# A table of expert gates in another memory layout: long runs where it is read, 256-byte pieces where it is written

## The reference, cut to what matters

```
s1, i1 = top_k(s[:, :, 0], 16);  s2, i2 = top_k(s[:, :, 1], 16)   # two keys of 128 each
sc, ic = top_k(s1[..., :, None] + s2[..., None, :], 16)
idx  = e1 * 128 + e2                                   # expert number
gate = softmax(sc)
act  = gelu(einsum('td,thkd->thk', xb, u[idx]))
out  = einsum('thk,thkd->td', gate * act, v[idx])
```

## Time and profile before

| | us |
|---|---|
| median of 3 runs (lowest, highest) | 4213.85 (4208.09, 4213.94) |
| the profiled execution, its own time | 4209.01 |
| its span, first to last instruction | 4207.4 |
| PE busy (share of the span) | 4016.6 (95%) |
| DVE busy | 3169.2 (75%) |
| ACT busy | 1439.4 (34%) |
| POOL busy | 1307.2 (31%) |

### The profile page before, as it was taken

How to read it: one execution, slowest core, us unless ns; L and a number is a source line. 1 busy time by engine, 2 the same in 40 slices (tenths; PEclk the granted TensorE clock), 3 DMA queues, 4 the chain that set the end, 5 groups by cost and what they waited for, 6 DMA issues and landing times.

```text
span 4207.4 us, 82817 instructions
## 1 busy us (share of the span) xinstructions
PE 4016.6 (95%) x30898; PEld 3663.9 (87%) x30898; DVE 3169.2 (75%) x6289; ACT 1439.4 (34%) x2563; POOL 1307.2 (31%) x1014
## 2 busy tenths in 40 slices
PE   8999999997689999999999998999999999999998
PEld 5998887786559979888888878999999999999997
DVE  5721424555762378887889888999999999999998
ACT  4212222223552132333378872222222222222223
POOL 5333331000121100344433324434434334444341
PEclk9999999999889999999999999999999999999999
DMA  6765675574833311344446669999999999999995
GB/s 223 228 200 192 204 241 191 227 264 127 231 115 96 125 54 39 103 143 144 142 153 206 222 222 337 298 301 300 302 302 301 300 299 300 300 300 301 303 300 191
DMA packets 532581, 928.46 MB, mean 221 GB/s; under 512 B 286849, under 2 KB 355201, under 8 KB 524817
## 3 DMA queue, kind: packets, MB, share of 16 engines
q1 hardware_dynamic: 396512, 549.91, 40.7%
q0 software_dynamic: 81056, 346.96, 24.6%
q10 hardware_dynamic: 54816, 28.85, 2.4%
HBM read 786.05 MB, written 206.30 MB: 236 GB/s over the span
## 4 chain that ended last, share of the span: by engine, by line
PE 42%; DMA 3%; DVE 2%; ACT 2%; SPq 1%; issue 0%; DVEq 0%; ACTq 0%
PE ex_pso L3728 19%; PE ex_psa L2951 19%; PE wte_psa L2951 3%; DMA eg_u<-in_u 2%; PE wt_ps L3468 1%; DVE wt_one L3417 1%; DVE wt_stage L3429 0%; ACT eg_u_high L3044 0%; DMA weights<-wt_stage 0%; ACT wt_one L3496 0%; ACT wt_stage L3503 0%; DVE wt_one L3421 0%; ACT eg_act L3071 0%; SPq L3378 0%; ACT wt_one L3495 0%
## 5 line engine op out<-in xcount | busy, mean ns | idle before, releaser
L3696 POOL DMA_INDIRECT ex_rows<-expert_rows,ex_here x512 | 588.4, 1149 | 953.5 <-DVE acc_tok L3936 864.0
L3936 DVE SCALAR_TENSOR_TENSOR acc_tok<-ex_rows,ex_wsp,acc_tok 128x1024 f32<-128x1024 f32 x512 | 635.1, 1283 | 0.0
L2951 PE MATMUL ex_psa<-x_dense_high,eg_u_high 128*128 128x288 f32 x2048 | 604.4, 295 | 7.1 <-DVEq L4050 6.3
L2951 PE MATMUL ex_psa<-x_dense_low,eg_u_high 128*128 128x288 f32 x2048 | 604.5, 295 | 0.0
L2951 PE MATMUL ex_psa<-x_dense_high,eg_u_low 128*128 128x288 f32 x2048 | 604.2, 295 | 0.0
L3050 POOL TENSOR_TENSOR eg_u_low<-eg_u,eg_u_high 128x1024 fp32r<-128x1024 f32 x130 | 314.2, 2417 | 742.1 <-ACT eg_u_high L3044 742.1
L3815 ACT ACTIVATE ex_w<-ex_psa 128x288 f32<-128x288 f32 x256 | 105.2, 411 | 1057.3 <-PE ex_psa L2951 1057.3
L3728 PE MATMUL ex_pso<-ex_w_high,ex_v_high 128*128 128x288 f32 x2048 | 442.4, 298 | 18.2 <-DVE acc L3918 16.6
L3728 PE MATMUL ex_pso<-ex_w_high,ex_v_low 128*128 128x288 f32 x2048 | 440.5, 297 | 0.0
L3728 PE MATMUL ex_pso<-ex_w_low,ex_v_high 128*128 128x288 f32 x2048 | 439.1, 296 | 0.0
L3918 DVE TENSOR_TENSOR acc<-ex_pso,acc 128x576 f32<-128x576 f32 x512 | 375.4, 754 | 44.8 <-PE ex_pso L3728 44.8
(11 more groups left out here) (577 smaller groups left out, 8799.2 us busy)
## 6 DMA issues: line engine op xcount, KB each, us to landing
eg_u<-in_u SPq DMA_DIRECT2D x256, 512.0 KB, 5.6
expert_rows<-in_v SPq DMA_DIRECT2D x128, 512.0 KB, 7.0
ex_v<-in_v SPq DMA_DIRECT2D x128, 512.0 KB, 6.4
weights<-wt_stage SPq DMA_DIRECT2D x36, 1024.0 KB, 4.9
ex_g<-weights SPq DMA_DIRECT2D x128, 288.0 KB, 6.7
expert_rows<-eg_act SPq DMA_DIRECT2D x256, 128.0 KB, 1.7
proj<-in_out POOLq DMA_DIRECT2D x50, 548.5 KB, 6.4
in_w<-in_w_in SPq DMA_DIRECT2D x50, 512.0 KB, 5.1
```

The costliest lines, as they stand in the source:

```text
L2951: yield nc.tensor.matmul(out[:, 0:b - a], w[:, kc, :], half[:, kc, a:b], start=n == 0, stop=n == len(passes) - 1)
L3696: pool.indirect_dma_start(rows[i][:, :], None, table, index(here[par][:, t, j:j + 1]), element_offset=ROW_RUNS[t][0]).then_inc(s_row[i], 16)
L3936: v.scalar_tensor_tensor(out=acc_tok[:, t, :], in0=rows[i][:, at:at + D], scalar=wsp[:, i:i + 1], in1=acc_tok[:, t, :], op0=ALU.mult, op1= ...
```

## The change

The table `weights` in memory was (token block, e2, e1, token) and becomes (e2, e1, token block, token). A load of one group's gates for one partition was 9 runs of 256 bytes, and is one run of 2304 bytes. A stored piece for one partition was one run of 8192 bytes, and is 32 runs of 256 bytes that lie 2304 bytes apart. The bytes moved and the number of DMA instructions are the same, and on every engine the instructions keep their places: 36 stores and 128 loads change their shape.

```
@@ store_piece
-                    sp.dma_start(io["weights"][b][:, f, :].rearrange("e f t -> e (f t)"),
-                                 stage[slot][:, f, :].rearrange("p f t -> p (f t)")).then_inc(s_st[slot], 16)
+                    sp.dma_start(io["weights"][:, f, b, :], stage[slot][:, f, :]).then_inc(s_st[slot], 16)
@@ load_gates
-                        sp.dma_start(g[s][:, :, :], io["weights"][:, :, sl, :].rearrange("b p e t -> p b (e t)")).then_inc(s_g[s], 16)
+                        sp.dma_start(g[s][:, :, :].rearrange("p b t -> p (b t)"), io["weights"][:, sl, :, :].rearrange("p e b t -> p (e b t)")).then_inc(s_g[s], 16)
@@ program
-                            ("weights", (NTB, NK, NK, TB)), ("expert_rows", (NK, NK, ROW))):
+                            ("weights", (NK, NK, NTB, TB)), ("expert_rows", (NK, NK, ROW))):
```

## The result

| | before | after |
|---|---|---|
| median, us | 4213.9 | 4256.38 |
| lowest to highest, us (4 runs each) | 4208.09 to 4219.23 | 4249.62 to 4258.13 |
| ratio, 95% interval | | 1.0098, 1.0082 to 1.0114 |
| profiled execution's span, us | 4207.4 | 4256.0 |

The change makes the kernel 42.5 us slower where 27 were forecast. The time lies in the stated range. The two spans differ by 48.6 us, and ACT's gelus divide them. The one ahead of the first stored block comes 3.6 us later after (2175.34 and 2178.98); 3.0 of these are there already at 2036 us, where the change has no part. From it to the last gelu of gate building it is 333.4 us before and 375.1 after, 41.7 more. From there to where PE runs without a break (2573.20 and 2621.77) it is 64.5 and 67.7, 3.2 more. Behind that nothing differs.

The account below looks back on a forecast made before the run. PE was taken to bound the loop and gate building. A loss of 24 us in gate building plus 2.7 in the transition, on the median 4213.9, gave 4241 us, range 4213 to 4268.

Parts of the forecast that it names:

- The steady loop: The loop after the transition: PE waits for nothing in 25.5 us a pair of groups, so shorter loads give nothing.
- A piece takes 2.3 us more: Stores in gate building and transition: 1.05 MB in 256-byte runs takes 4.8 us instead of 2.5.
- The DMA share: In gate building, the DMA share was to rise from 0.65 to about 0.85.
- ACT's waits: In gate building, ACT's wait for `eg_u` was to grow from 20.2 to about 55 us.
- PE's loss: In gate building, PE loses 3.7 us a block, 3.0 more than before; 24 us over eight blocks.
- the lead of 1.9: In gate building, DVE runs 1.9 us ahead of PE, which is taken off the delay that reaches PE.
- The transition: From gate building to the loop: it ends 2.7 us later, bounds 0 to 9.2.
- two terms of 9.2 and 6.5: In the transition, the four last pieces take 9.2 us more; DVE's idle of 6.52 us goes.
- The range: Whole kernel 4213 to 4268 us; the forecast's own range 4224 to 4268 allowed stage 10 to 45, transition 0 to 9.
- The rule on packets of queues taking turns: In the transition, loads' small packets alternate with gathered packets, so `eg_u` lands after 31.84 us; under 10 after the change.
- The estimate of 3.4 us for a piece: By the skill's descriptor cycles, a stored piece takes 0.9 us more and the kernel's sum is near no change.

Follow-up runs that it names:

- the runs with one late turn: Kernel before with only piece 0, or only piece 3, of each block stored twice in long runs: 4213.44 us and 4224.76 us.
- double_fourth: Kernel before with only piece 3 of each block stored twice in long runs: 4224.76 us, ratio 1.0045.
- double_store: Kernel before with each of the 32 pieces of gate building stored twice in long runs: 4255.01 us, ratio 1.0107.
- loads_alone: Kernel before with only the loads changed to one 2304-byte run per partition, stores still 8192-byte runs: 4203.24 us, ratio 0.9983.

## Why the prediction was right, and where its sizes were off

- **The steady loop: nothing.** Right: 3013 matmuls in 400 us before and after, at a DMA share of 0.88.
- **A piece takes 2.3 us more, and `eg_u` is there 9.6 us after the gelu.** Right: the two loads of the rows above are there 9.5 us (2337.10) and 10.2 us (2345.01) after the end of the gelu ahead of their issue (2327.60 and 2334.79), and the landing of `eg_u` has its median at 7.9 us (5.6 before), the forecast's number. The median of a piece is 6.6 us (4.8 before, 6.8 forecast). The DMA share did not follow: 0.85 was forecast and it is 0.69 in the block shown.
- **ACT's waits.** Forecast 2.4, 2.5, 0 and 1.9 us in turns 1 to 4; measured 2.7, 2.8, 0.5 and 1.7; in all 61.3 us (about 55 forecast).
- **PE's loss: the mis-sized term.** "Less the lead of 1.9" made it 0.8, 2.2 and 0.7 us in turns 1, 2 and 4; it was 1.8, 2.6 and 1.1, and 0.3 in turn 3. For the stage 24 us were forecast and 41.7 came. The lead had been read as DVE's wait less PE's, 2.51 - 0.59. The 0.59 counts from the end of the matmul record before, and these records run 0.39 us though one starts every 0.23. The weight load of the same matmul had waited longer:

```profile
2324.86 0.39 PE L2951 MATMUL wte_psa<-x_gathered_low,eg_u_high 128*128 128x512 f32 x1
2325.09 0.39 PE L2951 MATMUL wte_psa<-x_gathered_high,eg_u_low 128*128 128x512 f32 x1
2326.07 0.53 PEld L3468 LDWEIGHTS wt_ps<-wt_one 128*128 128x128 f32 x4 [1.02 <-DVE wt_one L3417]
```

That gives 1.5, and the means of all blocks before give 2.4 - 1.2 = 1.2 us; the runs with one late turn have 1.4 and 1.0. With 1.2 in the forecast's own sum, turn 1 would have lost 1.5, turn 2 2.2 and turn 4 1.1, less the 1.3 lost before (not 0.7): 3.5 a block, 28 us. So the lead is a small part of the miss. DVE's waits, up to 0.4 us longer in turns 1 and 2 than forecast, and turn 3, which lost 0.3, bring the weight loads' waits to what the table has: 4.6 us a block more than before, 36.7 in the stage.
- **The clock: a term that the sum did not have.** The gelus drift by 5.2 us a block, 0.6 more than those waits. Windows of the stage before, the stage after, and a stretch of it, with the matmuls there:

```profile
2175.34:2508.70 333.36, 327.13 (x1656) 274.54 (x1655) 298.44 (x634) 289.38 (x729) 112.98 (x47) 1.00 0.63 212
2178.98:2554.07 375.09, 338.70 (x1656) 278.96 (x1655) 298.67 (x634) 289.06 (x728) 112.36 (x47) 0.98 0.67 188
2247.50:2251.00 3.50, 3.50 (x11) 2.76 (x11) 2.85 (x7) 1.89 (x6) 0.06 (x1) 0.51 0.80 252
```

```profile
2246.98 0.78 PE L3467 MATMUL wt_ps<-wt_one 128*128 128x256 f32 x4 [2.38 <-DVE wt_one L3416]
2247.56 0.62 PE L2951 MATMUL wte_psa<-x_gathered_high,eg_u_high 128*128 128x512 f32 x1
2247.98 0.63 PE L2951 MATMUL wte_psa<-x_gathered_low,eg_u_high 128*128 128x512 f32 x1
```

Before, the granted clock was 1.00 all through the stage. After, it stood at 0.5 (1.2 GHz) in five stretches, each beside a wait of PE of 2.4 to 3.1 us; the longest such wait before was 1.4. In these stretches 29 matmuls of the early groups start 0.43 us apart instead of 0.23: 5.7 us, 0.7 a block, about what was left over. The same sum nearly closes the other runs: weight loads' waits and slow matmuls give 16.7 + 2.1 for 19.0 us in double_fourth and 35.9 + 8.0 for 45.7 in double_store. That PE's waits bring the clock down is read from rows that lie together; other waits of over 2 us had no such stretch beside them, and no run varied the clock alone.
- **The transition: 2.7 us, by two terms of 9.2 and 6.5.** The sum was 3.2, and the terms were others. DVE's first row slot came 13.0 us later, not 9.2, since SP's held issue kept every engine back, which the forecast did not have: SP had issued the last piece 17.75 us after the last gelu (5.16 before), 12.6 later. The pieces themselves landed 7.1 us later (2578.79 less 2554.07, the issue of the gates' load less the last gelu, against 17.6). DVE's own stretch gave back 9.8 us, not 6.5: the prediction called it free of other gaps, and it had five waits for gathered rows, 2.7 us in all, which went too. With them PE's waits for DVE's adds fell from 16.6 to 6.7 us, where the prediction had them stay. The two errors nearly cancel. That is luck, and the right sum proves neither term.
- **The range.** The time lies in it, but with the stage at 41.7 us of the 45 that it allowed; its centre was too low.
- **The rule on packets of queues taking turns.** In loads_alone the `eg_u` of the earlier trace rows is used 9.1 us after its issue (2537.68 to 2546.78) instead of landing after 31.84, DVE's idle of 6.52 us is gone, and the transition is 3.5 us shorter. The trace agrees with the Trainium skill (DMA: Bandwidth & Descriptors, "Queues, rings and completion order"), by which an engine takes turns between the queues packet by packet; the turns themselves are not seen in a row.
- **The estimate of 3.4 us for a piece**, worked out from the same page's cycles per descriptor ("Why small descriptors are slow"), is 308 GB/s, near the stretch at 290 and far from the one at 218. The kernel did not come out near no change, as the sum by that page had it.

## What to carry to other kernels

A transfer's price is not only its own time: look at what is queued behind it, and at who waits for that. Here four pieces a block, for which nobody waits, made the loads behind them land 2.3 us later; that cost 5.2 us a block, and moving one line of the issue order gave it all back and more. Before making a load in a PE-bound loop cheaper, ask which wait ends last there; before making a store dearer, measure the slack of the chain behind it, and read it from the weight load's wait, not from the matmul's. When the engine that sets the pace begins to wait, look at its granted clock too: here 5.7 of 41.7 us went there.

## What the runs showed of the hardware that was not expected

- Stores in 256-byte runs ran at two steady rates in one stretch, 290 and then 218 GB/s (14.1 and 18.8 ns a packet and engine), both with packets under 512 bytes of one queue alone. The times of the packets add up to 127.5% of the engines' span in 2561 to 2565 us and to 85.6% in 2567 to 2571. 512-byte runs had 347 GB/s. What switches between the rates was not tried.
- SP is through with a DMA of 4096 runs after 0.38 us, but is then held 3.9 us at the next DMA, and 15.3 us over four in a row; with 128 runs each it was 2.7 us. What holds it no row names. At the end of a part of the program this holds the other engines too: ACT starts 0.90 us after SP's last issue, before and after.
- TensorE's granted clock was at 0.5 in five stretches of the changed kernel's stage, each beside a wait of PE of 2.4 to 3.1 us, and never in the stage before.
